# Row halves instead of column halves in the experts' second product, and activations turned one chunk later for small experts

## What is computed

```
def moe_swiglu(x, w_router, w_gu, w_down):
    logits = x @ w_router                                  # 512 x 8
    top_val, top_idx = lax.top_k(logits, 2)
    gates = softmax(top_val)                               # two experts per token
    for e in range(8):
        g, u = split(x @ w_gu[e], 2)                       # 1024 -> 2 x 704
        out += gate[e] * ((silu(g) * u) @ w_down[e])       # 704 -> 1024
```

## Time and profile before

| | us |
|---|---|
| median of 3 runs (lowest, highest) | 1408.54 (1405.68, 1411.75) |
| profiled execution, own time | 1415.48 |
| its span | 1413.8 |
| PE busy | 1308.8 (93%) |
| DVE busy | 623.3 (44%) |
| ACT busy | 552.4 (39%) |
| POOL busy | 149.5 (11%) |
| mean granted TensorE clock | 0.963 |

### The profile page before, as it was taken

How to read it: one execution, slowest core, us unless ns; L and a number is a source line. 1 busy time by engine, 2 the same in 40 slices (tenths; PEclk the granted TensorE clock), 3 DMA queues, 4 the chain that set the end, 5 groups by cost and what they waited for, 6 DMA issues and landing times.

```text
span 1413.8 us, 17461 instructions
## 1 busy us (share of the span) xinstructions
PE 1308.8 (93%) x6511; PEld 1098.7 (78%) x6512; DVE 623.3 (44%) x829; ACT 552.4 (39%) x743; POOL 149.5 (11%) x106
## 2 busy tenths in 40 slices
PE   7999999899999999999899999988799899988658
PEld 6889987688888878867786899847687789767547
DVE  4334445433333332336533554446533642455475
ACT  3235533533223322234332333243545544556532
POOL 0000000000000000000000000000433433345400
PEclk9999999999999999999999999998899999989769
DMA  6331122233333433203356332214765866588831
GB/s 181 94 101 45 45 70 80 60 90 101 96 100 89 132 91 102 76 30 105 90 90 66 84 48 59 82 30 155 250 200 179 288 217 200 184 265 278 304 149 60
DMA packets 197911, 175.45 MB, mean 124 GB/s; under 512 B 7200, under 2 KB 178272, under 8 KB 197856
## 3 DMA queue, kind: packets, MB, share of 16 engines
q1 hardware_dynamic: 194016, 160.53, 39.4%
q0 software_dynamic: 3312, 12.06, 2.3%
q10 hardware_dynamic: 528, 2.10, 0.4%
HBM read 164.71 MB, written 9.96 MB: 124 GB/s over the span
## 4 chain that ended last, share of the span: by engine, by line
PE 84%; DVE 4%; issue 4%; DMA 3%; ACT 3%; POOL 1%; ACTq 0%; SPq 0%; POOLq 0%; DVEq 0%
PE bank L707 26%; PE bank L708 25%; PE bank L709 25%; DMA raw<-moe_w_down 2%; PE bank L804 2%; DVE w_lo L1612 1%; POOL w_lo L665 1%; DMA x_tok<-x 1%; ACT w_hi L1500 1%; PE bank L1017 1%; PE bank L945 0%; PE bank L884 0%; DVE het_lo L1640 0%; PE bank L797 0%; PE bank L796 0%
## 5 line engine op out<-in xcount | busy, mean ns | idle before, releaser
L1612 DVE TENSOR_TENSOR w_lo<-raw,w_hi 128x1024 fp32r<-128x1024 f32 (+5 forms) x215 | 300.9, 1406 | 302.9 <-ACT w_hi L1213 145.8
L707 PE MATMUL bank<-x_hi,w_hi 128*128 128x512 f32 x672 | 265.1, 394 | 12.2 <-DVE x_lo L1716 4.3
L708 PE MATMUL bank<-x_lo,w_hi 128*128 128x512 f32 x672 | 263.4, 392 | 0.0
L709 PE MATMUL bank<-x_hi,w_lo 128*128 128x512 f32 x672 | 263.1, 392 | 0.0
L1213 ACT CAST w_hi<-raw 128x1024 fp32r<-128x1024 f32 (+2 forms) x141 | 149.7, 1061 | 143.6 <-PE bank L709 135.9
L707 PE MATMUL bank<-w_hi,x_hi 128*128 128x256 f32 (+2 forms) x608 | 190.1, 313 | 6.7 <-DVE x_lo L1640 3.1
L708 PE MATMUL bank<-w_lo,x_hi 128*128 128x256 f32 (+2 forms) x608 | 187.2, 308 | 0.0
L709 PE MATMUL bank<-w_hi,x_lo 128*128 128x256 f32 (+2 forms) x608 | 187.2, 308 | 0.0
L707 PEld LDWEIGHTS bank<-x_hi,w_hi 128*128 128x128 f32 x672 | 127.1, 189 | 43.6 <-DVE w_lo L1612 10.2
L1500 ACT CAST w_hi<-raw 128x1536 fp32r<-128x1536 f32 (+2 forms) x98 | 130.1, 1340 | 75.5 <-PE bank L709 39.7
L709 PEld LDWEIGHTS bank<-x_hi,w_lo 128*128 128x128 f32 x672 | 127.3, 189 | 26.7
(11 more groups left out here) (307 smaller groups left out, 1815.1 us busy)
## 6 DMA issues: line engine op xcount, KB each, us to landing
raw<-moe_w_gu SPq DMA_DIRECT2D x32, 768.0 KB, 5.3
raw<-ffn_w_gu SPq DMA_DIRECT2D x44, 512.0 KB, 3.8
raw<-moe_w_gu SPq DMA_DIRECT2D x32, 640.0 KB, 4.1
raw<-a_w_qkv SPq DMA_DIRECT2D x24, 512.0 KB, 3.8
raw<-moe_w_down SPq DMA_DIRECT2D x16, 768.0 KB, 6.0
raw<-ffn_w_down SPq DMA_DIRECT2D x16, 704.0 KB, 4.4
raw<-ple_w_gate SPq DMA_DIRECT2D x16, 512.0 KB, 3.8
raw<-kvf_w SPq DMA_DIRECT2D x16, 512.0 KB, 7.6
```

What stands on the lines that cost most here:

```text
L707: pe.matmul(o, s_hi, m_hi, start=start, stop=False, skip_group_check=True)
L708: pe.matmul(o, s_hi, m_lo, start=False, stop=False, skip_group_check=True)
L709: return pe.matmul(o, s_lo, m_hi, start=False, stop=stop, skip_group_check=True)
L1612: return dve.tensor_tensor(dst, a, b, ALU.subtract)
```

## The change

The weights of the second product come by row halves: chunks 8 and 9 are rows 0 to 383 of both column halves, chunks 10 and 11 the other rows. Chunks 8 and 9 then need only half 0 of the activations, and chunks 10 and 11 complete the two result banks. The piece of the last 64 rows moves from chunk 9 to chunk 10, so chunk 9 is 1536 elements wide in place of 1024 + 512 of 64 rows, and chunk 10 the reverse. For experts of one or two tiles, PE turns half 0 behind chunk 5 (before: 4) and half 1 behind chunk 9 (before: 8); ACT's steps follow, so that for half 1 its cast of the next expert's chunk 0 moves in front of `het_hi`, for every expert. The results of these experts go to banks 0 to 3, and the copies to `y_tok` now come behind chunks 10 and 11.

```
+def out_bank(half, t, n):
+    return half * (2 if n <= 2 else 4) + t
 SP:
-                    full, r0, col = (3, 2)[c % 2], c % 2 * 3 * P, c // 2 * 512
+                    full, r0, col = (3, 2)[c // 2], c // 2 * 3 * P, c % 2 * 512
-                    if c % 2:
+                    if c >= 2:
 PE:
-            def second_half(t, c):
+            def second_half(t, c, n):
-                    kk = c % 2 * 3 + k
+                    kk = c // 2 * 3 + k
-                    mm = mm3(bank[4 * (c // 2) + t][:, :], het_hi[0:r, kk, t * P:(t + 1) * P],
+                    mm = mm3(bank[out_bank(c % 2, t, n)][:, :], het_hi[0:r, kk, t * P:(t + 1) * P],
-                            pe.wait_ge(banks_out, 8 * e + 4)
+                            pe.wait_ge(banks_out, 8 * e + (4 if n <= 2 else 8))
-                        if c == 4:
+                        if c == (5 if n <= 2 else 4):
                             turn_hidden(e, 0, n)
                     for t in range(n):
-                        mm = second_half(t, 0)
+                        mm = second_half(t, 0, n)
                     mm.then_inc(chunk_done, 1)
+                    if n <= 2:
+                        expert_weights(e, 9)
+                        for t in range(n):
+                            mm = second_half(t, 1, n)
+                        mm.then_inc(chunk_done, 1)
                     turn_hidden(e, 1, n)
-                    for c in range(1, 4):
+                    for c in range(2 if n <= 2 else 1, 4):
 ACT:
-                if c in (9, 11):
+                if c >= 10:
-                    for c in range(9):
+                    for c in range(10):
                         deep_hi(e, c + DEEP - 1)
-                        if c in (4, 8):
-                            hidden_hi(e, c // 8, n)
+                        if c in (5 if n <= 2 else 4, 9):
+                            hidden_hi(e, c // 9, n)
-                    for c in range(1, 4):
+                    for c in range(2, 4):
                         deep_hi(e, 8 + c + DEEP - 1)
-                        if c % 2:
-                            act.wait_ge(chunk_done, 4 * q0 + 12 * e + 8 + c + 1)
+                        act.wait_ge(chunk_done, 4 * q0 + 12 * e + 8 + c + 1)
 DVE:
-                if c == 9:
+                if c == 10:
-                        if c in (4, 8):
+                        if c in (5 if n <= 2 else 4, 8):
                             turned_lo_parts(e, c // 8, n)
```

More of the change, by code:

```diff
@@ L572, in _ @@
                                      ).then_inc(raw_loaded[c], 16)
[L573 removed]
+                    if c >= 2:
                         src = moe_w_down[0][bass.ds(e, 1), (KE - 1) * P:FE, col:col + 512]
                         sp_eng.dma_start(raw[c][0:FE_LAST, 1024:1536], src.rearrange("e p n -> (e p) n")
[L576 removed]
+                                         ).then_inc(last_loaded[c - 2], 16)
             def gate1_step(q, i, j, last):
@@ L663, in third_low @@
                 pool.wait_ge(hi_ready, L0 + 12 * e + c + 1)
-                j, n = c % DEEP, 4 * FC[c // 4] if c < 8 else (1536, 1024)[c % 2]
+                j, n = c % DEEP, 4 * FC[c // 4] if c < 8 else (1536, 1024)[(c - 8) // 2]
                 op = pool.tensor_tensor(w_lo[j][:, 0:n], raw[j][:, 0:n], w_hi[j][:, 0:n].bitcast(F32), ALU.subtract)
@@ L1157, in body @@
                     turn_x(e + 1, after)
-                    for c in range(1, 4):
+                    for c in range(2 if n <= 2 else 1, 4):
                         expert_weights(e, 8 + c)
-                        if c == 2:
+                        if c == 1:
                             pe.wait_ge(xg_ready, TT * e + 2 * TT)
                         for t in range(n):
-                            mm = second_half(t, c)
+                            mm = second_half(t, c, n)
                         mm.then_inc(chunk_done, 1)
@@ L1498, in deep_hi @@
                 act.wait_ge(chunk_done, 4 * q + j + 1 - DEEP)
-                n = 4 * FC[c // 4] if c < 8 else (1536, 1024)[c % 2]
+                n = 4 * FC[c // 4] if c < 8 else (1536, 1024)[(c - 8) // 2]
                 op = act.copy(w_hi[j][:, 0:n], raw[j][:, 0:n])
-                if c in (9, 11):
-                    act.wait_ge(last_loaded[c // 2 % 2], 16 * e + 16)
+                if c >= 10:
+                    act.wait_ge(last_loaded[c - 10], 16 * e + 16)
                     op = act.copy(w_hi[j][0:FE_LAST, 1024:1536], raw[j][0:FE_LAST, 1024:1536])
@@ L1529, in body @@
                 def body(n):
-                    for c in range(1, 4):
+                    for c in range(2, 4):
                         deep_hi(e, 8 + c + DEEP - 1)
-                        if c % 2:
-                            act.wait_ge(chunk_done, 4 * q0 + 12 * e + 8 + c + 1)
-                            for t in range(n):
-                                act.copy(y_tok[:, t, c // 2 * 512:(c // 2 + 1) * 512],
-                                         bank[4 * (c // 2) + t][:, :]).then_inc(banks_out, share(t, n))
+                        act.wait_ge(chunk_done, 4 * q0 + 12 * e + 8 + c + 1)
+                        for t in range(n):
+                            act.copy(y_tok[:, t, c % 2 * 512:(c % 2 + 1) * 512],
+                                     bank[out_bank(c % 2, t, n)][:, :]).then_inc(banks_out, share(t, n))
                 by_tiles(act, count_e, body)
```

## The result

The changed kernel took 1422.68 us (median of 4 runs, 1420.3 to 1430.59), against 1407.11 us for the kernel before beside it (4 runs, 1404.81 to 1411.75): a ratio of 1.0098, 95% interval 1.0066 to 1.0131. Run again later in another group (e5_after_again) it took 1426.21 us against 1407.58, ratio 1.0136 (1.0099 to 1.0173). So it is 15.6 us slower in one group and 18.6 in the other, and the forecast of +5 us, like the range up to 1420, was too low.

A forecast was written before the change was run, and what follows sets the result against it. PE bounds two-tile experts; one-tile experts wait on the feed of loads, casts and POOL. Terms 0 - 0.5 + 0 + 0.6 + 5 = +5.1 gave 1408.5 + 5 = 1413.5 us, range 1403 to 1420.

The forecast's parts named there:

- Half 0 later, gain 0: One-tile experts before chunk 8: 7.9 us of `he` waits go but return as waits for POOL; gain 0.
- Half 1 behind a cast that waits: One-tile experts before chunk 10: `het_hi` stands behind the next chunk 0's cast, which waits for its load; 3.4 us after landing.
- Expert 7, +5: Last expert: `het_hi` waits for the gate weights, PE stops some 9 us before chunk 10; +5, from +2.5 to +5.4.
- The bound of 7.6: Last 18 second-product matmuls of a one-tile expert: 7.6 us at 0.42 us each when nearly all run at half clock.
- Expert 2, 0: Expert 2: chunk 10 at 1117.1, end 1121.8 to 1124.7, before 1122.1; 0, from -0.3 to +2.6.
- -0.5 and +0.6: Changes for experts 5 and 6: -0.5 (from -3.4 to -0.5) and +0.6 (from -1.1 to +1.8).
- It is at half clock now, so I take -0.5: Expert 5: end 1261.4 to 1264.3, before 1264.8; already at half clock in the profile used, so -0.5 taken.
- against medians: 1408.5 + 5 = 1413.5: Whole kernel: the +5 us is added to a median before that lies 7 us below the profiled time.
- the clock at chunk 10 in every one-tile expert: Rival, start of chunk 10: the stop drops the clock, all 18 remaining matmuls at half rate; 1418, chance 0.27.
- The removed waits stay removed: Rival, one-tile experts: `he` waits gone for good, chunk 8 earlier, clock full; 1384 to 1397, chance 0.10.
- The last expert's stop is hidden: Rival, expert 7: gate weights land by the end of the transposes; sum 0.1, time 1408.5, chance 0.15.
- the signs that the forecast had named for being wrong: Chunk 8 of experts 5 to 7 under 18 us, expert 7 under 37 us, or clock 1.00 in experts 5 and 6.

The follow-up runs named there:

- e3: The kernel before, with only half 0 turned behind chunk 5 for one- and two-tile experts: 1408.59 us, ratio 1.0015.
- e1: The changed kernel with ACT's cast of the next expert's chunk 0 moved back behind `het_hi` of half 1: 1407.05 us, ratio 0.9992 to the kernel before.
- e4: The kernel before, unchanged, profiled once more: 1409.65 us, ratio 1.0003, profiled span 1405.0 us.
- e11: The kernel before, unchanged, one more profile: a single execution of 1406.14 us, span 1404.5 us.
- e6: The changed kernel with the final stage's loads issued behind the third chunk of the last gate product: 1413.43 us, ratio 1.0034 to the kernel before.
- e9: Row halves, half 1 turned behind chunk 8 again, POOL and DVE exchanging low-part chunks, two steps moved ahead of a wait: 1414.49 us, ratio 1.003 to the kernel before.
- e12: The changed kernel, unchanged, one more profile: a single execution of 1425.18 us, span 1423.5 us.
- e10: The changed kernel with `het_hi` ahead of the next chunk 0's cast and the final loads issued later: 1407.53 us, ratio 0.9982 to the kernel before.

## Why the prediction was wrong, step by step

- **Half 0 later, gain 0: right.** The wait for POOL became 15.1 us, "about 15" had been said; e3 shows the exchange by itself. Chunk 8 of experts 5, 6 and 7 started 19.2, 19.6 and 19.7 us after the expert's start, not under 18.
- **Half 1 behind a cast that waits: right in its mechanism.** The row of `he` vanished, `het_hi` stands directly behind the 1536-wide cast that waited for its load, and e1 shows that this order is the whole loss. The Trainium skill (TensorE: Matmul & The Clock Gate, the queue depths in "Architectural detail: the array is 16x 32x32, not 1x 128x128") says that ScalarE takes its queue strictly in order; the traces agree: in expert 7 of the changed kernel `het_hi` comes behind 7.95 us of ACT's wait for the gate weights, though its transposes had ended at 1323.0, and in e1 it waits for its transposes alone.
- **Expert 7, +5: the stop was right, the rest short.** Forecast was a stop of "some 9 us", measured 9.42. But the load landed after 13.2 us in place of 12.3, chunk 10 started 36.3 us after the expert's start in place of 35.1, and the last 18 matmuls took 8.7 us in place of 4.7 to 7.6. The expert took 44.9 us, the forecast's upper bound was 1341.6 - 1298.9 = 42.7. The bound of 7.6 was mis-sized: its 0.42 us per matmul came from the earlier trace rows, a stretch with a mean clock of 0.58, in which the last matmuls ran at full clock. Behind the stop they took 0.48 us each at a clock of 0.52, and in expert 5, where chunk 10 came just when forecast (29.1 us after the expert's start), 8.9 us for 18 made +0.8 out of -0.5.
- **Expert 2, 0: too low.** It grew by 1.5 us (its clock went from 0.95 to 0.90), within the bound of +2.6. Experts 5 and 6 grew by 0.8 and by nothing, where -0.5 and +0.6 had been said. The four together are +9.9 us where +5.1 had been said, the whole mixer is +8.7 (353.4 in place of 344.7), but it began 3.0 us earlier (988.5 in place of 991.5) and what lies behind its end was 0.9 us shorter (76.7 in place of 77.6). This made the profile's difference look right, +4.8 us, and that was luck.
- **The step that failed: "It is at half clock now, so I take -0.5", and with it "against medians: 1408.5 + 5 = 1413.5".** The change was charged against one execution, 1415.48 us and thus 7 us above its own median, and that excess was carried over as if it belonged to both kernels alike. It doesn't. Experts 5 to 7 were 8 us longer in it than in e4 and e11, in the very stretches that the change touches, and 7 of these were PE's busy time at half clock. There the changed kernel could not lose what had been lost already. Against e4 and e11 experts 5 to 7 grow by 13.4 to 19.9 us, and the profiled spans by 13.6 to 19.0; expert 5 alone by 2.0 to 5.3 in place of -0.5, expert 7 by 9.7 to 10.6 in place of +5. In all three profiles of the changed kernel chunk 10 of experts 5 and 7 began at half clock, behind stops of 3.84 to 4.37 and 9.19 to 9.55 us. In the kernel before, chunk 9 of expert 5 did so in one profile of three, behind 1.51 us.
- **The rivals.** The slower one, the clock at chunk 10 in every one-tile expert (1418, 0.27), was the nearest and named a mechanism that is a large part of the loss (below); it too was worked out against the longer profile and is 5 to 8 us too low. Its place isn't quite right: chunk 10 started at half clock in experts 5 and 7, but in expert 6 at full clock in all three profiles, behind stops of 2.34, 2.13 and 3.32 us. "The removed waits stay removed" is refuted by e1: with the stop gone the time is still that of before. "The last expert's stop is hidden" was the right lever, shown by e6, but not what the changed kernel does.

None of the signs that the forecast had named for being wrong came: chunk 8 of experts 5 to 7 was not early, expert 7 took more than 37 us, and the clock was not 1.00. They test the mechanism, and none of them tests the baseline that it was charged against.

How the loss divides: e6 takes away 9 to 13 us by shortening expert 7's long wait, and e1 all of it. The table above separates standing still from half clock for experts 5 to 7, since both kernels run the same matmuls there. Against e4 and e11 PE's idle time grows by 7.3 to 8.1 us, much the same in every profile, and its busy time by 5.5 to 12.0 us, which is the clock's part and varies from one execution to the next. The stretch behind the mixer gives a little back: it took 76.7 to 78.8 us in the changed kernel's profiles, 80.2 and 81.1 in e4 and e11.

## What to carry to other kernels

Before a sum is made against one profiled execution, compare its own time with the median: if it is above, look for where the excess lies, and if that is where the change acts, charge the change against the undisturbed state as well. When a step is moved back in an in-order engine's queue, look at what it moves behind: a cast that waits for a load holds up what stands behind it by what is left of the load's landing (3.2 us in expert 5, more than 7 in expert 7 here, for landings of 6.3 and 13.2 us). And where several inputs of an engine are late by about the same amount, removing the wait for one, as e1 and e9 do, only shows the wait for the next.

## What the runs showed of the hardware

- **Half clock after stops of 1.1 to 2.4 us, and not each time.** In front of chunk 9 of expert 6 PE stood 1.31 us in the kernel before and went on with a matmul of 0.79 us; in e4, at the same place, it stood 1.11 us and went on at full clock, but behind a stop of the same 1.11 us in expert 7 at half clock. In e9 a stop of 2.75 us ended at full clock, in e12 one of 3.32 us too, in e10 one of 2.36 us at half. The rows of e4:

```profile
1282.83 0.49 PE L707 MATMUL bank<-w_hi,het_hi 128*128 128x512 f32 x1 [1.11 <-DVE het_lo L1640]
1316.45 0.79 PE L707 MATMUL bank<-w_hi,het_hi 128*128 128x512 f32 x1 [1.11 <-DVE het_lo L1640]
```

  That of e9:

```profile
1285.39 0.49 PE L715 MATMUL bank<-w_hi,het_hi 128*128 128x512 f32 x1 [2.75 <-DVE het_lo L1649]
```
  And that of e10:

```profile
1279.13 0.79 PE L717 MATMUL bank<-w_hi,het_hi 128*128 128x512 f32 x1 [2.36 <-POOL w_lo L675]
```

  So the length of the one stop doesn't decide it, and the runs don't show what does.
- **One execution of the same program can be 8 us longer than another, 7 of them by half clock** (the table above). The last group's 23 runs of the kernel before went from 1403.15 to 1417.44 us around a median of 1408.99.
- **A load's landing depends on the traffic around it.** The 512 KB of gate chunk 0 took 12.3 and 13.2 us with the final loads ahead of it on SP's queue, and 5.7 us with these issued behind it (e6).
